# A three-pass down projection as eleven 4-block units, and the same projection as Strassen's seven block products

## What is computed

```python
h2 = rms_norm(x, g_norm_ffn[l]) * (1.0 + sc2) + sh2
u_gate, u_val = jnp.split(h2 @ w_up[l], 2, axis=-1)          # 2 x 2816 columns
u_gate = causal_dwconv(u_gate, conv_w[l], conv_b[l])         # 3 taps along the tokens
x = x + (1.0 + gt2) * ((jax.nn.gelu(u_gate) * u_val) @ w_down[l])   # 512x2816 @ 2816x1024
return rms_norm(x, g_final)
```

## Time and profile before

| | |
|---|---|
| Median of 3 runs | 933.62 us (932.97 to 934.3) |
| Span of the profiled execution | 932.2 us |
| TensorE busy | 908.2 us (97%), 4454 matmul records |
| VectorE, ScalarE, GpSimd busy | 449.5, 368.6, 446.2 us |

### The profile page before, as it was taken

The page is one execution under the profiler, slowest core; times in us unless marked ns, Lnnn a source line. Parts: engine busy times, 40 slices in busy tenths (PEclk is TensorE's granted clock), DMA queues, the critical chain, the costliest instruction groups (busy, mean ns, idle before and its releaser), DMA issues.

```text
span 932.2 us, 11736 instructions
## 1 busy us (share of the span) xinstructions
PE 908.2 (97%) x4454; PEld 767.6 (82%) x4454; DVE 449.5 (48%) x716; ACT 368.6 (40%) x491; POOL 446.2 (48%) x396
## 2 busy tenths in 40 slices
PE   3999999999999999999999999999999999999996
PEld 3788898988888888888888888888888888888885
DVE  4846678675558988976625436222222222200005
ACT  5534425252444324353322338444444444422114
POOL 2589534354333442444554545544444444444445
PEclk9999999999999999999999999999999999999999
DMA  9932221212443777345426231322332222332212
GB/s 314 288 124 91 91 91 55 82 46 91 135 137 122 239 226 227 123 148 178 163 91 226 92 103 37 131 90 90 104 116 95 90 90 90 94 133 90 91 46 91
DMA packets 94087, 115.52 MB, mean 124 GB/s; under 512 B 2206, under 2 KB 84314, under 8 KB 94046
## 3 DMA queue, kind: packets, MB, share of 16 engines
q1 hardware_dynamic: 94046, 114.95, 37.3%
HBM read 112.81 MB, written 2.13 MB: 123 GB/s over the span
## 4 chain that ended last, share of the span: by engine, by line
PE 42%; issue 29%; POOL 23%; SPq 3%; DVE 1%; DMA 1%; ACT 1%; POOLq 0%; DVEq 0%; ACTq 0%
PE bank L1100 41%; POOL w_lo L686 20%; SPq L528 2%; DMA w_raw<-in_w_in_dram 1%; POOL masks L623 1%; POOL masks L660 1%; SPq L534 1%; SPq L502 0%; POOL w_lo L700 0%; DVE xn_ffn L1970 0%; POOL masks L658 0%; SPq L523 0%; DVE h_tmp2a L1624 0%; ACT h_tmp L803 0%; DVE x L2061 0%
## 5 line engine op out<-in xcount | busy, mean ns | idle before, releaser
L686 POOL TENSOR_TENSOR w_lo<-w_raw,w_hi 128x512 fp32r<-128x512 f32 x292 | 390.4, 1368 | 437.0 <-ACT w_hi L769 432.4
L1100 PE MATMUL bank<-h_hi,w_hi 128*128 128x512 f32 (+1 forms) x880 | 339.7, 389 | 0.1
L1100 PE MATMUL bank<-h_lo,w_hi 128*128 128x512 f32 (+1 forms) x880 | 337.2, 386 | 0.3 <-POOL h_lo L667 0.2
L1100 PE MATMUL bank<-h_hi,w_lo 128*128 128x512 f32 (+1 forms) x880 | 261.1, 386 | 0.0
L769 ACT ACTIVATE w_hi<-w_raw 128x2048 fp32r<-128x2048 f32 x72 | 137.6, 1911 | 217.8 <-PE bank L1100 217.8
L1100 PEld LDWEIGHTS bank<-h_lo,w_hi 128*128 128x128 f32 x880 | 165.2, 188 | 33.8 <-POOL h_lo L667 1.2
L1100 PEld LDWEIGHTS bank<-h_hi,w_lo 128*128 128x128 f32 x880 | 165.3, 188 | 33.1
L1100 PEld LDWEIGHTS bank<-h_hi,w_hi 128*128 128x128 f32 x880 | 165.1, 188 | 32.7 <-POOL h_lo L673 0.3
L1100 PE MATMUL bank<-w_lo,act_hi 128*128 128x512 f32 x176 | 68.5, 389 | 0.0
L1100 PE MATMUL bank<-w_hi,act_hi 128*128 128x512 f32 x176 | 68.5, 389 | 0.0
L1100 PE MATMUL bank<-w_hi,act_lo 128*128 128x512 f32 x176 | 68.5, 389 | 0.0
(11 more groups left out here) (259 smaller groups left out, 1131.2 us busy)
## 6 DMA issues: line engine op xcount, KB each, us to landing
w_raw<-in_w_in_dram SPq DMA_DIRECT2D x32, 1024.0 KB, 5.2
w_raw<-in_w_up_dram SPq DMA_DIRECT2D x22, 1024.0 KB, 5.1
ada<-in_w_ada_dram SPq DMA_DIRECT2D x16, 1024.0 KB, 5.3
w_raw<-in_w_down_dram SPq DMA_DIRECT2D x11, 1024.0 KB, 4.8
ada<-in_w_ada_dram SPq DMA_DIRECT2D x16, 512.0 KB, 8.6
w_raw<-in_w_out_dram SPq DMA_DIRECT2D x4, 1024.0 KB, 5.0
x_in<-in_x_dram SPq DMA_DIRECT2D x4, 512.0 KB, 5.1
w_raw<-in_w_in_dram SPq DMA_DIRECT2D x8, 256.0 KB, 7.2
```

Source lines behind the costliest of these rows:

```text
L686: ins = pool.tensor_tensor(wlo[slot][:, cols], raw[slot][:, cols], whi[slot][:, cols].bitcast(F32), ALU.subtract)
L1100: return pe.matmul(o, lhsT, rhs, start=start, stop=stop, **kw)
```

## The change

The down projection is one product of a 512 x 2816 matrix and a 2816 x 1024 matrix. Each step's 256 x 512 piece of activations (features x tokens) and 256 x 1024 piece of weights is seen as 2 x 2 blocks: two halves of the features (e, o), two halves of the tokens (0, 1), and for the weights two k-blocks and two column halves. Seven products of sums of blocks replace eight of the blocks themselves; a product here is two token tiles, three passes, one 128 x 512 block of weights for each step.

- Two products (numbers 3 and 4) need blocks of the activations as they are (`own`) and differences of weight blocks. They are done in the up loop: `first_down(i)`, 12 matmuls between gate(i+1) and val(i+1). For it SP loads a down unit into `dn_raw` (when `dn_used` says that the last one is used), VectorE subtracts (`down_differences`), ScalarE rounds (`high_down`) and GpSimd writes two low parts (`low_down`).
- Three products (1, 5, 7) follow the loop as "slots" n = 0 to 10, and two (2, 6) as n = 11 to 21. A slot has its own three (or two) blocks of weights, six places in turn: SP loads, VectorE adds blocks (`slot_sum`), ScalarE rounds (`high_slot`), GpSimd writes two low parts (one from n = 11) and VectorE one (`low_slot` on both).
- In the up loop VectorE no longer writes `act_lo`. It writes the sums of activation blocks (`mixes`, four instructions), the low part of `own`, and of three mixed blocks (`low_own`, `low_mix`). The sums for products 2 and 6 are kept whole and are split in three parts during the slots (`high_mix2`, `low_mix2`).
- The results are combined after the products: ScalarE copies products 3 and 4 into `y_sum`, VectorE adds and subtracts 1, 5, 2 (`product_1`, `product_5`, `product_2`) and finishes each half tile with three instructions instead of two (`finished`). Product 6 uses the banks of product 1, product 2 those of 4, product 7 those of 3.
- The last four slots run token tile by token tile. The gate row and the final gain are loaded later than before, and the order in which half tiles are finished is `LAST_ORDER`.

The core of the diff, in the order SP, GpSimd, ScalarE, TensorE, VectorE:

```diff
+PRODUCTS = {1: ((0, 1), 0), 5: ((2, 3), 0), 7: ((4, 5), 1), 3: ((4, 5), 0), 4: ((6, 7), 0), 2: ((6, 7), 1), 6: ((0, 1), 1)}
+FIRST, SECOND = (3, 4), ((1, 5, 7), (2, 6))
+SLOTS = 6
...
+            def load_slot(n):
+
+                raw_, got, i = sl_raw[n % SLOTS], landings[n % SLOTS], n % STEPS
+                if n >= SLOTS:
+                    sp.wait_ge(sl_used, n - SLOTS + 1)
...
+            load_up(0)
+            load_up(1)
+            load_down(0)
+            with sp.Fori(1, STEPS - 1) as i:
+                load_up(i + 1)
+                sp.wait_ge(dn_used, i)
+                load_down(i)
...
-            with pool.Fori(0, (N_UNITS - U_UP) // 2 - 1) as i:
+            def low_down(i):
+
+                pool.wait_ge(dnhi_done, i + 1)
+                for b in range(2):
+                    ins = pool.tensor_tensor(dn_lo[:, b, :], dn_raw[:, 512 * (b + 1):512 * (b + 2)],
+                                             dn_hi[:, b, :].bitcast(F32), ALU.subtract)
+                ins.then_inc(dnlo_done, 1)
...
+            with pool.Fori(0, STEPS - 1) as i:
                 low_part(2 * i + U_UP + 2, 0)
                 low_part(2 * i + U_UP + 3, 1)
-            low_part(N_UNITS - 1, 0)
+                low_down(i)
...
+            first_tap(0)
+            with act.Fori(0, STEPS - 1) as i:
+                high_part(0, 8 * (U_UP + 4) + 16 * i)
+                gelus(i)
+                high_down(i)
+                up_over(act, "val", i)
                 high_part(1, 8 * (U_UP + 4) + 16 * i)
-            for u in range(U_DOWN + 2, N_UNITS):
-                unit_high(u)
+                high_own(i)
+                high_mix(i)
+                act.wait_ge(own_lo_done, i + 1)
+                first_tap(i + 1)
...
+            def first_down(i, start, stop):
+
+                pe.wait_ge(own_lo_done, i + 1)
+                pe.wait_ge(dnlo_done, i + 1)
...
+            def up_and_down(i, start):
+
                 up_tiles("gate", 0, i + 1)
+                first_down(i, start, False)
                 up_tiles("val", 1, i + 1)
...
+            def slot_product(n, q, j):
+
+                s_, i, order = n % SLOTS, n % STEPS, products_of(n)
+                b = {1: 2, 5: 1, 7: 0, 2: 0, 6: 1}[q]
+                pe.wait_ge(sllo_done[q in (7, 6)], n + 1)
+                if i == 0:
+                    claim(pe, ("P", q, j))
...
+            for j in range(2):
+                for q in SECOND[1]:
+                    for n in range(2 * STEPS - 4, 2 * STEPS):
+                        slot_product(n, q, j)
...
+            def finished(q, j, t, half):
+
+                b, cols = ready(dve, ("P", q, j)), slice(512 * half, 512 * half + 512)
+                link(tt(b[:, :], b[:, :], y_cols(t, half), ALU.add))
+                link(tt(b[:, :], b[:, :], g2_row[:, cols], ALU.mult))
+                tt(x1[:, t, cols], x1[:, t, cols], b[:, :], ALU.add).then_inc(x2_done, 1)
...
+            with dve.Fori(0, STEPS - 1) as i:
+                taps(i)
+                down_differences(i)
+                gate_times_value(i)
+                up_written(i)
+                mixes(i)
+                low_own(i)
+                low_mix(i)
...
+            for n in range(3, 2 * STEPS):
+                slot_sum(n)
+                low_slot(n - 1)
+                if n in (9, 12, 16):
+                    low_mix2((9, 12, 16).index(n))
+                if n == 14:
+                    product_1(0)
+                    product_1(1)
+                    dve.wait_ge(gate_in[1], 16)
+                if n == 15:
+                    product_5(0)
+                if n == 16:
+                    product_5(1)
+                if n == 17:
+                    finished(7, 0, 0, 0)
+                if n == 18:
+                    finished(7, 1, 1, 0)
```

More of the change, by code:

```diff
@@ L365, in layer_kernel @@
         c_in, vec_in = sem("c_in"), sem("vec_in")
-        ada_in = [[sem(f"ada_in{j}_{half}") for half in range(2)] for j in range(KT // 2)]
+        landings = [sem(f"landings{i}") for i in range(2 * (KT // 2))]
         pair_done = sem("ada_pair_summed")
@@ L440, in evacuated, with up_over, landed, products_of @@
             eng.wait_ge(free[b], n + 1)
+        def up_over(eng, name, i=STEPS - 1):
+            b, n = BANKS[f"{name}1"]
+            eng.wait_ge(full[b], i + (n + 1))
+        def landed(n):
+            return 32 + sum(32 if m < STEPS else 16 for m in range(n % SLOTS, n + 1, SLOTS))
+        def products_of(n):
+            return SECOND[0] if n < STEPS else SECOND[1]
+        def rows_after(t, half):
+            return LAST_ORDER.index((t, half)) + 1
         def h_part(k):
@@ new lines, in _ @@
+            load_up(0)
[5 more added lines that the diff above has]
+                load_down(i)
+            sp.wait_ge(lo_done, U_DOWN - 1)
+            load_slot(0)
+            sp.wait_ge(lo_done, U_DOWN)
+            load_slot(1)
+            up_over(sp, "gate")
+            load_slot(2)
+            sp.wait_ge(dn_used, STEPS - 1)
+            load_down(STEPS - 1)
+            up_over(sp, "val")
@@ L2043, in _, with mixes, sums, one @@
-                    tt(lo, gelu[:, t, :], hi.bitcast(F32), ALU.subtract).then_inc(alo_done, 1)
+                    bk, n = BANKS[f"val{t}"]
+                    dve.wait_ge(free[bk], i + (n + 1))
+            def mixes(i):
+                (e0, e1), (o0, o1) = ([gated_up[:, t, 256 * j:256 * j + 256] for j in range(2)] for t in range(2))
+                def sums(slots):
+                    return mix[:, slots, bass.ds(i, 1), :].rearrange("p c a s -> p c (a s)")
+                def one(tile):
+                    return tile[:, bass.ds(i, 1), :].rearrange("p a s -> p (a s)")
+                tt(sums(slice(0, 4, 3)), gated_up[:, 0, :].rearrange("p (j s) -> p j s", j=2),
+                   o1.unsqueeze(1).broadcast_to([P, 2, 256]), ALU.add)
+                tt(one(mix[:, 1, :, :]), e0, o0, ALU.add)
+                tt(one(mix[:, 2, :, :]), o0, o1, ALU.subtract)
+                tt(one(mix2[1]), e1, e0, ALU.subtract).then_inc(mix_done, 1)
@@ new lines, in _ @@
+            slot_sum(1)
+            taps(i)
+            slot_sum(2)
+            low_slot(0)
+            low_slot(1)
+            down_differences(i)
+            gate_times_value(i)
+            up_written(i)
+            mixes(i)
+            low_own(i)
+            low_mix(i)
+            for n in range(3, 2 * STEPS):
+                slot_sum(n)
[14 more added lines that the diff above has]
+                    finished(7, 1, 1, 0)
```

336 lines of the change are left out of this document (248 added, 88 removed).

## The result

The changed kernel takes **943.39 us** (median of 4 runs, 942.5 to 945.73), the kernel before 933.41 beside it: ratio 1.0109, 95% interval 1.0094 to 1.0124. It is slower by 1.1%; the forecast was 942.3.

What follows compares the result with a forecast made beforehand. TensorE, busy 97% of the span, bounds the kernel. Matmuls -15.0, up loop +10.0, slots +12.2, tail +1.5 make +8.7 us on the 932.2 span: 940.9, plus 1.4 for the median: 942.3 us; range 929 to 948.

Steps and rivals of the forecast that it cites:

- Matmuls and pace: Down projection: 462 matmuls instead of 528, pace unchanged at 0.2267 us each, 15.0 us less.
- The turns: GpSimd and VectorE, both on SBUF inputs, alternate by instruction; GpSimd pays 0.45 us beside 512 columns, VectorE about 1.07 each time.
- the price line: GpSimd's added time beside a VectorE SBUF instruction: 0.18 us for 256 columns, 0.45 for 512, 0.72 for 768, 1.00 for 1024.
- Steps 2 to 9: Up loop: TensorE waits 0.6 us a step for GpSimd's down blocks, 4.8 us over eight steps; 25.1 us a step.
- The tenth wait: Behind the ninth up step, `slot_sum(0)` also delays GpSimd's last instruction: TensorE waits 1.6 us.
- The first step: Up loop: first down load queues behind the value load, lands at 588.8; TensorE waits 3.6 us for GpSimd (2 to 5).
- case C: Rival: TensorE's wait in slot 11 drops its clock to 1.2 GHz, costing 1.5 to 3 us: 945 us; chance 0.10.
- The slots: After the up loop: VectorE's queue with turns makes TensorE wait 12.2 us, about 5.7 in slot 11, 5.7 at slots 20 and 21.
- The tail: After the last matmul: a third instruction in `finished` and later roots on ScalarE add 1.5 us (0.7 to 3).
- A: Rival, loop and slots: covers hold, turns hardly coincide or VectorE's lead hides them; -10.0 us, 923.6 us; chance 0.15.
- B: Rival: up steps have just room enough, slots lose half (6.5 us); -3.4 us, 930.2 us; chance 0.13.

Runs made afterwards that it cites:

- experiment 1: Changed kernel with GpSimd's low parts of the down blocks moved between those of the gate and value units: 933.6 us, ratio 0.9998.
- experiment 3: Changed kernel with VectorE alone writing all low parts of the slots, GpSimd none: 944.04 us, ratio 1.0101.
- experiment 4: Changed kernel with product 1 combined behind slot sum 12, two slots earlier: 946.84 us, ratio 1.014.
- experiment 5: Changed kernel with GpSimd writing both low parts of slots 11 to 17, VectorE none there: 945.52 us, ratio 1.012.
- experiment 6: Changed kernel without VectorE's `low_mix`; ScalarE writes that block by plain copy, so values are not the reference's: 937.97 us, ratio 1.0035.
- experiment 7: Changed kernel with 12 extra matmuls on TensorE before its first-step wait for the down blocks, their result overwritten: 942.9 us, ratio 1.0089.
- experiment 12: Changed kernel with the last four slots run slot by slot like the others: 945.4 us, ratio 1.013.
- experiment 2: Changed kernel with the first down load issued ahead of the loads of up step 1: 939.19 us, ratio 1.0049.
- experiment 9: Changed kernel with the two up-loop edits of experiment 1 and experiment 2 together: 931.91 us, ratio 0.9977.
- experiment 10: Kernel of experiment 9 with VectorE alone writing all low parts in slots 3 to 13: 925.3 us, ratio 0.991.
- experiment 11: Kernel of experiment 10 with VectorE's combining and mix parts reordered, and GpSimd writing both low parts of slots 14 and 15: 922.16 us, ratio 0.9883.

## Why the prediction was right, step by step

**Matmuls and pace:** right, 4388 records for 4454, each 0.2267 us apart where nothing waits.

**The turns:** right, also where no row of before had the size: 1.47 and 2.00 us for the 0.18 and 0.72 us of the price line (1.29 + 0.18, + 0.72). The Trainium skill's rule of an exclusive lock on the shared ports (SBUF — State Buffer, Who interferes with whom) agrees with these rows in that the two engines take turns. A turn as long as the whole other instruction would have made 1.90 us (1.29 + 0.61) beside 512 columns; the row has 1.74.

**Steps 2 to 9:** right. 25.04 us a step (681.58 to 706.62, the starts in two steps) against the 25.1 forecast. The tenth wait is 1.43 us against 1.6.

**The first step:** the mechanism right, the size off. The term that was mis-sized is the second megabyte: forecast 8.0 us from issue to landing (5.1 + 2.9), measured 9.6 (581.36 to 590.94), and it was issued 0.6 us later than forecast. GpSimd was 0.5 us quicker than forecast with what follows. The forecast left out that a third megabyte, for gate(2), is issued while the second is on its way:

```profile
586.68 0.39 SPq L563 DMA_DIRECT2D w_raw<-in_w_up_dram  x1
```

The size also varies from one execution to the next. In the traces that share this code the load takes 7.9 to 9.2 us (experiments 1, 3 to 7 and 12) and the wait is 3.65 to 4.28 (3, 4, 5, 6 and 12), so the change's profile shows a long one, and the 3.6 forecast is near the others.

**The clock:** the step that was missing from the sum. What case C describes came, in slot 11 and also in the first step, where C did not look for it, and it was given one chance in ten beside the forecast rather than a place in it. In the first step its 2.5 us delay all of TensorE's work up to the slots; experiment 7 shows that a part of such a delay is made good there. In slot 11 its 3.0 us are not an extra: from the first matmul of product 6 to that of slot 19 it is 22.31 us in the change (900.19 to 922.50), and 22.30 in experiment 2 (893.31 to 915.61), where the same matmuls ran at full clock and waited 2.0 us longer before slot 19. VectorE has no idle time from 888.5 to 926.3 in the change: it is VectorE's work that makes that stretch as long as it is.

**The slots:** 12.2 us forecast, 10.85 lost (7.3 of waits, 3.0 of half clock, the rest restarts). The places were right but one, the sizes by place were not. The 5.7 us of slot 11 before product 6, for VectorE's L2350, are 3.01, and 1.61 us stand at slot 10 instead, for GpSimd, behind the first `low_mix2`. The 5.7 us of slots 20 and 21 are 2.7 us of waits before slots 19 to 21, and the 3.0 us of half clock that went by before them. VectorE went from the low part of slot 9 (886.30) to the sum of slot 21 (end 922.9) in 36.6 us against 38.7; its instructions show six turns with GpSimd in it instead of eight, and two turns at 1.07 us are that difference.

**The tail:** +1.86 against +1.5. It is not a fixed size: with the same instructions behind the last matmul, the traces of experiments 2, 4, 5 and 7 have 8.3 to 8.4 us from there to the end, some 0.8 more than before, and that of experiment 1 has 9.4.

So the forecast's +8.7 us stands against +10.0 of the medians. It is right by its mechanism, and that it came so close is in part luck: the half clock of the first step (2.5) was missed, and the slots were 1.3 us too dear. The term of the slots is not a fixed size either: with the same order of work in them and less lost in the loop they lost 10.6 us in experiment 1, but 12.4, 13.0, 12.5 and 13.3 in 2, 6, 7 and 9. In these four the matmuls behind the waits before slots 19 to 21 ran at half clock, in the change and in experiment 1 they did not. **The rivals:** A and B asked for covers that hold. In the loop they would have held with one call in another place (experiment 1), which I had not looked for; the prediction took the order of GpSimd's queue for given and asked only whether its length fits. In the slots they would not have.

What stays open: how much the order of the last four slots is worth, why the median of experiment 6 fell by 1 to 2 us more than its waits, and what makes a wait lower the clock in one execution and not in another.

## What to carry to other kernels

When an engine writes several things in a loop, its queue should have them in the order in which the consumer asks: the same ten instructions in another order made the median some 10 us shorter. Two engines that take turns at SBUF did best here when one of them did a stage's work alone and the other had its turn where its partner works from PSUM (experiment 10); splitting each slot between them gave 3.97 us a slot against 2.8. Where an engine is busy without a break, moving its work earlier moved the wait (experiment 4); what helped was to put behind the last urgent item what only the tail needs (experiment 11, though the tail grew by 1 us for it).

## What the runs showed of the hardware

**The clock behind a wait.** In the change a wait of 5.08 us was followed by 12 matmuls at half speed, one of 2.86 by 14. But in experiment 2 the same wait before product 6 was followed by none. Stretches of that kernel, the wait and what follows:

```profile
890.30:893.20 2.90, 0.15 (x1) 1.00 0.51 181
893.30:898.00 4.70, 4.30 (x18) 1.00 0.30 101
```

The Trainium skill (TensorE: Matmul & The Clock Gate, Why this matters for your kernels) names idle gaps between bursts of matmuls as what lowers the clock. The change's trace agrees, and experiment 7, with 1.49 us of idle time in place of 5.08, has full clock there. Experiment 2 shows that the same idle time can also pass without it, so this is a cost that a wait may or may not have. Shorter waits can have it too: in experiment 10 it was 1.80 and 0.73 us of idle time, 1.7 us apart, ahead of 14 matmuls at half speed, while the change had 0.76, 0.73 and 0.72 in the same place ahead of none. The clock does not explain why the times of the change spread over 3.2 us and those of the kernel before over 1.3: the mean granted clock was 0.989 in the longest (945.73) and in the shortest (942.5).

**Loads on their way together.** A megabyte lands 5.1 us after its issue in the median of the up loads. Of two issued 0.4 us apart, with a third 5.3 us later, the first took 7.4 us in the change, the second 9.6 and the third 6.9; in the other traces with these three loads the second took 7.9 to 9.2. From 582 to 591 us the DMA engines were busy without a break and moved 343 GB/s, 3.1 MB: the three loads share that rate.
